# Sample states of a state-space stage: per head pair of four sequences instead of per sequence

## The reference

```python
chunk_states = einsum('bclgn,bcgel,bclgep->bcgepn', Bc, decay_to_end, xdt)
y_off        = einsum('bclgn,bcgepn,bcgel->bclgep', Cc, h_prev, exp(a_cum))
h_last       = h_prev * chunk_decay[..., None, None] + chunk_states
```

## Time and profile before

| | us |
|---|---|
| median of 3 runs | 1492.87 |
| lowest, highest run | 1485.05, 1494.22 |
| the profiled execution | 1489.72 |
| its span on the core | 1488.2 |

### The profile page before, as it was taken

One profiled execution on the slowest core, in us unless ns is written; L12 is line 12 of the kernel. 1 busy time (PEld: TensorE's weight loads), 2 busy tenths in 40 slices (PEclk: granted clock), 3 DMA queues, 4 the chain that ended last, 5 costly groups with the idle time before them and its releaser, 6 DMA issues. The chain is left out here.

```text
span 1488.2 us, 27180 instructions
## 1 busy us (share of the span) xinstructions
PE 1417.5 (95%) x10645; PEld 1332.1 (90%) x10645; DVE 822.6 (55%) x1194; ACT 654.4 (44%) x1086; POOL 222.4 (15%) x398
## 2 busy tenths in 40 slices
PE   4999999989989999999999999999999999999997
PEld 4998777888879988889988988899999999999997
DVE  3554545887742566777687675774444444442221
ACT  4565454766631354574364473434432333331221
POOL 3002232000021213322222213211100000000000
PEclk9999999999999999999999999999999999999999
DMA  3225674221256433434334425352223222223331
GB/s 116 72 78 169 177 213 146 67 61 59 67 126 195 97 92 109 113 103 114 101 114 109 114 72 177 109 191 71 86 71 88 81 85 85 85 81 100 95 93 48
DMA packets 201109, 157.35 MB, mean 106 GB/s; under 512 B 13672, under 2 KB 187216, under 8 KB 200959
## 3 DMA queue, kind: packets, MB, share of 16 engines
q1 hardware_dynamic: 175394, 97.93, 23.0%
q0 software_dynamic: 25232, 57.70, 13.5%
q10 hardware_dynamic: 384, 0.37, 0.1%
HBM read 132.04 MB, written 23.91 MB: 105 GB/s over the span
## 5 line engine op out<-in xcount | busy, mean ns | idle before, releaser
L449 PE MATMUL tile_banks<-x_hi,w_hi 128*128 128x288 f32 (+1 forms) x1808 | 530.9, 308 | 18.0 <-ACT gate_out L1723 14.0
L450 PE MATMUL tile_banks<-x_lo,w_hi 128*128 128x288 f32 (+1 forms) x1808 | 508.3, 296 | 0.0
L453 PE MATMUL tile_banks<-x_hi,w_lo 128*128 128x288 f32 (+1 forms) x1808 | 386.9, 295 | 0.0
L449 PEld LDWEIGHTS tile_banks<-x_hi,w_hi 128*128 128x128 f32 (+1 forms) x1808 | 341.9, 189 | 33.5 <-issue 25.3
L450 PEld LDWEIGHTS tile_banks<-x_lo,w_hi 128*128 128x128 f32 (+1 forms) x1808 | 342.1, 189 | 4.7 <-issue 3.6
L423 DVE TENSOR_TENSOR w_lo<-w_raw,w_hi 128x1024 fp32r<-128x1024 f32 (+2 forms) x169 | 208.3, 1233 | 174.7 <-ACT w_hi L417 173.5
L453 PEld LDWEIGHTS tile_banks<-x_hi,w_lo 128*128 128x128 f32 (+1 forms) x1808 | 291.4, 188 | 0.4
L417 ACT ACTIVATE w_hi<-w_raw 128x1024 fp32r<-128x1024 f32 (+2 forms) x169 | 175.7, 1039 | 103.6 <-PE tile_banks L453 102.0
L450 PE MATMUL tile_banks<-f_lo,w_hi 128*128 128x288 f32 x352 | 98.3, 295 | 0.0
L449 PE MATMUL tile_banks<-f_hi,w_hi 128*128 128x288 f32 x352 | 97.8, 294 | 0.0
L453 PE MATMUL tile_banks<-f_hi,w_lo 128*128 128x288 f32 x352 | 73.9, 291 | 0.0
(11 more groups left out here) (378 smaller groups left out, 2501.2 us busy)
## 6 DMA issues: line engine op xcount, KB each, us to landing
w_raw<-in_w_in SPq DMA_DIRECT2D x68, 512.0 KB, 3.8
w_raw<-in_w_gate SPq DMA_DIRECT2D x22, 512.0 KB, 3.8
w_raw<-in_w_up SPq DMA_DIRECT2D x22, 512.0 KB, 3.7
k_page<-in_cache_k SPq DMA_DIRECT2D x64, 128.0 KB, 2.6
v_page<-in_cache_v POOLq DMA_DIRECT2D x64, 128.0 KB, 3.0
old<-in_state_ssm POOLq DMA_DIRECT2D x32, 256.0 KB, 3.4
out_ssm_sample<-old POOLq DMA_DIRECT2D x32, 256.0 KB, 2.8
w_raw<-in_w_pb SPq DMA_DIRECT2D x16, 512.0 KB, 3.6
```

The lines of the kernel that those rows point to most:

```text
L449: nc.tensor.matmul(out, wh, xh[:, HALVES[h]], start=start and k == 0, stop=False, skip_group_check=onto)
L450: nc.tensor.matmul(out, wh, xl[:, HALVES[h]], start=False, stop=False, skip_group_check=onto)
L453: mm = nc.tensor.matmul(out, wl, xh[:, HALVES[h]], start=False, stop=stop and k == last, skip_group_check=onto)
```

## The change

The unit of the sample work is no longer one sequence b with 8 heads (4 pairs), but u = (half, j): one head pair j of the four sequences of a half (half = u // 4, j = u % 4). There are again 8 units a group, two in each chunk, and loads and stores follow: old[:, u % 2] holds head pair j of four sequences q.

- New states: one product, xend_s of that head pair stationary, all of b_seq (96 x 512) streaming.
- Old states: for each sequence q, the half's 32 token columns of C are stationary and old_t[:, q] (128x128) streams; the output (32 x 128) goes to partitions 32q to 32q + 31. It has tokens as rows and each sequence against all 32 tokens.
- ACT copies that 128x128 block to a new buffer y_seq (y_rows), TensorE transposes it (turn_y) into a new key ("y_turn", g, u), and DVE's copy to y_old picks each sequence's own 8 of 32 token columns.
- turn_y(2c) stands behind the gemm slices that follow sequences(2c), turn_y(2c + 1) behind the slices that follow sequences(2c + 1). There are 8 more bank uses a group; the order is now old_t, old_t, y_seq_old, new_state, y_turn, y_seq_old, new_state, y_turn.
- DVE does the multiply-adds first and the copy to y_old after them.

```diff
         state = sb("state", [P, HG * HD], F32, ssd)
-        old = sb("old", [P, 2, PG, P], F32, ssd)
-        old_t = sb("old_t", [P, 2, PG, P], F32, ssd)
+        old = sb("old", [P, 2, SEQS, P], F32, ssd)
+        old_t = sb("old_t", [P, 2, SEQS, P], F32, ssd)
         b_seq = sb("b_seq", [3 * ROWS, SEQS, P], F32R, ssd)
         y_old = sb("y_old", [P, PG, TS], F32, ssd)
+        y_seq = sb("y_seq", [P, P], F32, ssd)
         end_decay = sb("end_decay", [P, 5, NH], F32, ssd)
...
                     keys += [("old_t", g, b) for b in (2 * c, 2 * c + 1)]
-                    keys += [(what, g, b) for b in (2 * c, 2 * c + 1) for what in ("y_seq_old", "new_state")]
+                    keys += [(what, g, u) for u in (2 * c, 2 * c + 1) for what in ("y_seq_old", "new_state", "y_turn")]
             keys += [("state_out", g), ("y_ss", g, 0), ("y_ss", g, 1)]
...
             return conv_acc[:, k % 2, 0:T]
+        def states_of(dram, g, u):
+            half, j = u // PG, u % PG
+            h = g * HG + 2 * j
+            return dram[0, half * SEQS:(half + 1) * SEQS, h:h + 2].rearrange("b e p n -> (e p) b n")
...
                     eng.wait_ge(sem(f"state_stored{b % 2}"), 16 * (n // 2))
-                eng.dma_start(old[:, b % 2], state_ssm[0, b, g * HG:(g + 1) * HG].rearrange("(j e) p n -> (e p) j n", e=2)).then_inc(sem(f"state_in{b % 2}"), 16)
+                eng.dma_start(old[:, b % 2], states_of(state_ssm, g, b)).then_inc(sem(f"state_in{b % 2}"), 16)
...
                         wait_after_read(eng, ("new_state", g, b))
-                        eng.dma_start(ssm_sample[0, b, g * HG:(g + 1) * HG].rearrange("(j e) p n -> (e p) j n", e=2), old[:, b % 2]).then_inc(sem(f"state_stored{b % 2}"), 16)
+                        eng.dma_start(states_of(ssm_sample, g, b), old[:, b % 2]).then_inc(sem(f"state_stored{b % 2}"), 16)
                     if two in conv_keys_:
...
-            def sequence(g, b):
-                key = ("y_seq_old", g, b)
+            def sequences(g, u):
+                half, j = u // PG, u % PG
+                key = ("y_seq_old", g, u)
                 wait_read(pe, key)
-                wait_after_read(pe, ("old_t", g, b))
-                for j in range(PG):
-                    mm = pe.matmul(spare(key)[:, j * TD:(j + 1) * TD], old_t[:, b % 2, j, :],
-                                   bc_t[:, g % 2, 1, TP + b * TD:TP + (b + 1) * TD], start=j == 0, stop=True, skip_group_check=True)
+                wait_after_read(pe, ("old_t", g, u))
+                at = TP + half * ROWS
+                for q in range(SEQS):
+                    mm = pe.matmul(spare(key)[q * ROWS:(q + 1) * ROWS, 0:P], bc_t[:, g % 2, 1, at:at + ROWS], old_t[:, u % 2, q, :],
+                                   start=True, stop=True, skip_group_check=True)
                 mm.then_inc(bank_full[use[key][0]], 1)
-                key = ("new_state", g, b)
+                key = ("new_state", g, u)
                 wait_read(pe, key)
-                pe.wait_ge(sem("b_seq_made"), 2 * g + 1 + b // SEQS)
+                pe.wait_ge(sem("b_seq_made"), 2 * g + 1 + half)
                 pe.wait_ge(sem("xend_s_made"), g + 1)
-                for j in range(PG):
-                    mm = pe.matmul(spare(key)[:, j * P:(j + 1) * P], xend_s[:, b // SEQS, 2 * j:2 * j + 2, :].rearrange("p h d -> p (h d)"),
-                                   b_seq[:, b % SEQS, :], start=j == 0, stop=True, skip_group_check=True)
-                mm.then_inc(bank_full[use[key][0]], 1)
+                pe.matmul(spare(key)[:, :], xend_s[:, half, 2 * j:2 * j + 2, :].rearrange("p h d -> p (h d)"),
+                          b_seq[:, :, :].rearrange("p b n -> p (b n)")).then_inc(bank_full[use[key][0]], 1)
+            def turn_y(g, u):
+                key = ("y_turn", g, u)
+                wait_read(pe, key)
+                wait_after_read(pe, ("y_seq_old", g, u))
+                pe.transpose(spare(key)[:, 0:P], y_seq[:, :], ident[:, :]).then_inc(bank_full[use[key][0]], 1)
...
                     gemm(two, range(2, 4) if one else range(5, 6))
-                    sequence(g, 2 * c)
+                    sequences(g, 2 * c)
                     gemm(two, range(4, 6) if one else range(6, 7))
-                    sequence(g, 2 * c + 1)
+                    turn_y(g, 2 * c)
+                    sequences(g, 2 * c + 1)
                     gemm(two, range(6, 8) if one else range(7, 8))
+                    turn_y(g, 2 * c + 1)
                 before, later = plan[NC]
...
+            def y_rows(g, u):
+                wait_full(eng, ("y_seq_old", g, u))
+                n = g * NB + u
+                if n:
+                    wait_full(eng, ("y_turn", (n - 1) // NB, (n - 1) % NB))
+                eng.activation(y_seq[:, :], spare(("y_seq_old", g, u))[:, 0:P], ACT.Copy).then_inc(bank_read[use[("y_seq_old", g, u)][0]], 1)
             for key in before_groups[:-1]:
...
                         sequence(g, b)
+                    for u in (2 * c, 2 * c + 1):
+                        y_rows(g, u)
                     if two:
...
                     else:
-                        wait_after_read(eng, ("y_seq_old", g, NB - 1))
+                        wait_after_read(eng, ("y_turn", g, NB - 1))
                         link(eng.tensor_tensor(e, e, y_old[:, :, :], ALU.mult))
...
-            def sequence(g, b):
-                n = g * NB + b
-                key = ("y_seq_old", g, b)
+            def sequences(g, u):
+                half, j = u // PG, u % PG
+                key = ("new_state", g, u)
+                wait_full(eng, key)
+                for q in range(SEQS):
+                    b = half * SEQS + q
+                    ins = eng.scalar_tensor_tensor(out=old[:, u % 2, q, :], in0=old[:, u % 2, q, :], scalar=seq_decay[:, g * PG + j, b:b + 1],
+                                                   in1=spare(key)[:, q * P:(q + 1) * P], op0=ALU.mult, op1=ALU.add)
+                ins.then_inc(bank_read[use[key][0]], 1)
+                key = ("y_turn", g, u)
                 wait_full(eng, key)
                 if g:
                     eng.wait_ge(sem("y_added"), NC * g)
-                eng.tensor_copy(y_old[:, :, b * TD:(b + 1) * TD], spare(key)[:, 0:PG * TD].rearrange("p (j t) -> p j t", j=PG))\
+                own = spare(key)[:, 0:SEQS * (ROWS + TD)].rearrange("p (b s) -> p b s", b=SEQS)[:, :, 0:TD]
+                eng.tensor_copy(y_old[:, j, half * ROWS:(half + 1) * ROWS].rearrange("p (b t) -> p b t", b=SEQS), own)\
                    .then_inc(bank_read[use[key][0]], 1)
-                key = ("new_state", g, b)
-                wait_full(eng, key)
-                for j in range(PG):
-                    ins = eng.scalar_tensor_tensor(out=old[:, b % 2, j, :], in0=old[:, b % 2, j, :], scalar=seq_decay[:, g * PG + j, b:b + 1],
-                                                   in1=spare(key)[:, j * P:(j + 1) * P], op0=ALU.mult, op1=ALU.add)
-                ins.then_inc(bank_read[use[key][0]], 1)
...
                     for b in (2 * c, 2 * c + 1):
-                        sequence(g, b)
+                        sequences(g, b)
                     if two:
```

## The result

| | before | after |
|---|---|---|
| median of 6 runs, us | 1494.12 (1485.05 to 1496.16) | 1474.37 (1470.6 to 1475.24) |
| ratio, 95% interval | | 0.9872 [0.9851, 0.9892] |
| profiled execution, its span, us | 1489.72, 1488.2 | 1470.6, 1469.1 |

The account below looks back on a forecast made before the run. TensorE was taken to bound the kernel. Per call 0.69 + 0.24 + 0.05 + 0.18 = 1.16 us against 1.34, times 32 saves 5.8 us: 1483.9 from the profile, 1487.1 from the median, 1486 taken; range 1475 to 1497.

Parts of the forecast that it names:

- What bounds the stage: State-space stage, 535 to 970 us: TensorE never starved for long, so a microsecond of its work is nearly one of span.
- Work removed: TensorE, per sequence() call: old-state products 0.81, new-state products 0.48, leaving 0.05; 1.34 us, times 32 = 42.9 us.
- The old-state block: Four products on four 32-row strips: 0.59 us plus 0.10 entry, 0.69 us a call; bounds 0.37 and 1.02.
- my order: Old-state strips: a product's second pass waits for its first, next strip's first pass starts with it; 0.107 us a product.
- Rival A: Old-state block: all four strips run at once, 0.37 us; 16.0 us saved, 1477; chance 0.20.
- New states: One 512-column product in place of four of 128: 0.24 us against 0.48, plus 0.05 for leaving, per call.
- Turns: Transposing y_seq back on TensorE amid projection matmuls: 0.10 + 0.08 = 0.18 us per call.
- B: Old-state block: no overlap, strips' streams go one by one, 1.02 us; 4.8 us lost, 1498; chance 0.12.
- C: turn_y() becomes a wait: ACT or DVE late beyond 0.20 us of cover; 6.4 us eats the saving, 1493; chance 0.10.
- D: Split weights come no sooner, part of the gain becomes L423 waits; at most half the gain, 1490; chance 0.08.
- Transfers: State transfers keep 256 KB, 3.4 us; loads follow stores and multiply-adds, which come earlier as much as TensorE or more.
- the place that I called the tightest: Last group's short chunk: second load lands by 941.5, transposed from 942.39; 0.9 us over, claimed to stay.

Follow-up runs that it names:

- E3: Kernel before with old-state products streaming 128 columns in place of 8, output the same; 1491.7 us, ratio 0.9987 [0.9972, 1.0003].
- E5: Changed kernel with all four old-state products written to one strip (partitions 0 to 31), part of y not the reference's; 1494.75 us.
- E6: Changed kernel with the four old-state products written to two strips in turn, part of y not the reference's; 1481.36 us.
- E1: Kernel before with the new layout and one 512-column new-state product, old-state products as before; 1485.04 us, ratio 0.9948 [0.9927, 0.9969].
- E9: Changed kernel, unchanged, timed again for a second profile; 1477.83 us, ratio to the kernel before 0.9879 [0.9856, 0.9902].
- E7: Changed kernel with each chunk's first turn_y() directly behind its sequences(), ahead of the projection slice covering ACT's copy; 1477.35 us, ratio 0.989 [0.9865, 0.9915].
- E11: E1's kernel (new states alone, against the kernel before), unchanged, timed again for a second profile; 1479.52 us.

## Why the prediction was wrong

- **What bounds the stage: right.** What came off TensorE's list came off the stage: 14.1 us by the list, and 17.9 less the 3.4 of the clock, 14.5, by the stage.
- **Work removed: right.** 42.9 us worked out, 26.43 + 15.29 summed and 0.05 x 32 for leaving, 43.3. That the 8 streamed columns do not set the time was shown by E3.
- **The old-state block: the step that failed.** I took 0.69 us, with 0.10 of it for the entry; measured are 0.35 and 0.09, 0.44 in all, 0.25 us or 8.0 us over 32 calls. The wrong sentence is "a product's second pass waits for its first, and the next strip's first pass starts together with it". The pairs in the earlier trace rows were there because L1365 has two strips. With two strips my order and the simultaneous start of equal passes take the same time, 0.107 us a product, so the time of the block could not decide. The block's opening could, and I misread it. In my order one pass starts alone and two follow, three within the first 0.2 us; the earlier trace rows has four. Cut finer, L1365 in the kernel before, whose first record starts at 676.31:

```profile
676.32:676.33 0.01, 0.01 (x2) 0.01 (x2) 1.00 2.17 512
676.42:676.43 0.01, 0.01 (x2) 0.01 (x4) 1.00 0.00 0
676.47:676.48 0.01, 0.01 (x4) 0.01 (x4) 1.00 0.76 205
```

  Two passes are under way at once from the start, two more join after 0.16 us. E5, E6 and the changed kernel, one, two and four strips, settle it. Rival A's order was right and its price low: two passes of 0.107, 0.05 to drain and 0.10 to enter, 0.37 us, where 0.44 was measured, because the drain is some 0.13 and not 0.05. The Trainium skill (TensorE: Matmul & The Clock Gate, Part 3) states that matmuls on different array tiles run together from about 4 ns apart; the four starts here lie within 20 ns, which is some 7 ns apart, so they agree in kind. The second passes, 0.13 us later, are not in that rule.
- **New states: low.** 0.24 + 0.05 taken, 0.34 measured, 1.5 us over 32 calls. The 0.24 of the earlier trace rows was read ahead of a bf16 product. Ahead of a projection matmul E1 has 0.32, without any strip near it, so it is not the cost of leaving the strips either; and the extra 0.05 behind it is gone.
- **Turns: high.** 0.18 taken, 0.11 measured, 2.2 us over 32 calls: 0.20 less the entry of 0.09 ahead of the second block, and 0.03 with 0.08 on the product behind it at the chunk's end.
- **Sum.** By the measured terms 0.35 + 0.09 + 0.34 + 0.11 is 0.89 us a call against 1.34. From the forecast: 5.8 + 8.0 (block) - 1.5 (new states) + 2.2 (turns) = 14.5 us, which is what the stage shows without the clock. Rival A said 16.0.
- **The clock: not in the sum.** One fall, behind 916 us, is the 0.98 of the earlier trace rows's last stretch, which I quoted and took for nothing; the other, at 780, lies outside both stretches. Together they cost 3.4 us of the profiled 1489.72 and are absent in the first profile after. Over all runs the difference is 2.1 us (standard error 0.9), which, with 14.5, makes 16.6. The measured 19 to 20 has an interval of 16 to 22 and E9's 18 one of 15 to 22, so the last 1 to 3 us may be noise; no run shows where they are.
- **Luck.** With 14.5 us off the list and nothing else the time would have been 1494.1 - 14.5 = 1480, inside the range although the order of the passes and the size of the gain were wrong. That the measured time lies below it is the clock and what stays open.
- **Rivals B, C, D: rightly unlikely.** B's 1.02 us is what one strip takes (E5, 0.99 and the entry). C did not happen: no PE wait for y_seq, and E7 shows how much cover is needed. D did not: the waits for w_lo are 3.1 us before and after.
- **Transfers: the loads did not come earlier by as much as TensorE did.** At the place that I called the tightest 0.7 of the 0.9 us is left (issued at 921.38, 3.6 us to land, transposed from 925.73). One wait of 0.5 us appeared a chunk before it, in the changed kernel:

```profile
907.83 1.50 POOL L886 DMA_DIRECT2D old<-in_state_ssm  x2 [3.81 <-DMA out_ssm_sample<-old]
...
911.27 0.60 PE L1383 MATMUL spare_bank<-ident,old 128*128 128x128 f32 x4
...
912.38 0.63 PE L1383 MATMUL spare_bank<-ident,old 128*128 128x128 f32 x4 [0.50 <-DMA old<-in_state_ssm]
```

  In the kernel before the same loads were issued at 921.00 and transposed from 927.20. So TensorE arrives 15.9 us earlier, the loads, which wait for the stores, only 13.2. The prediction had compared a saving of 0.36 us a chunk; it was 0.9.

## What to carry to other kernels

When a row's timing can come from an order of instructions or from the number of units that share the work, ask what the row would look like with another number of units; if both readings fit, the forecast should stand between them and not on one. Before that, cut the row finer: the first starts of a block can tell two orders apart that take the same time. Small f32 products whose stationary operand is wide and whose stream is narrow were worth turning round here into strips even with a copy and a transposition added, as long as something else covers the copy; and strip work in one block gained another 3 us. A product's price depends on what stands behind it (0.24 us ahead of a bf16 product, 0.34 ahead of a projection matmul), and a new one can make its successor dearer: price both. Read the granted clock of each stretch before summing: a mean of 0.98 over some 100 us hides nearly 2 us.

## What was not expected of the hardware

- Equal passes of four f32 products on four 32-row strips start within 20 ns of each other, the second passes 0.13 us later: 0.99, 0.56 and 0.35 us for the same eight passes on one, two and four strips.
- A stream of 128 columns costs no more than one of 8 where 128 f32 columns must be loaded (26.29 and 26.43 us for 256 passes). The falls of the granted clock at 780 and 915 us were absent with the wide stream, and also in E1 and E11 without it.
- TensorE's granted clock fell in the kernel before in two stretches of 10 us in which it was busy for 9.76 and 10.00, 1.7 us lost each; in the changed kernel it fell in the stage in one profile and not in the other.
- A 128x128 f32 transposition costs 0.11 us beside strips and at a chunk's end alike; there 0.08 of it shows on the product behind it.
